# A second matmul front in split products: low parts by GpSimd, roots straight from PSUM

## The chip, the cores and the metric

The kernel runs on one core of one Trainium2 chip. The metric is the device time of one execution in microseconds. The kernel before was timed three times (2276.06, 2279.28 and 2283.34 us); the profile is of one more execution, which took 2286.72 us, of which the span of its instructions is 2284.9 us.

## The reference, cut to what matters

Two transformer layers run one after the other, all in fp32, on 256 tokens of width 1024. Each mixes the tokens and then sends them through an expert layer (PEER). The change is in the mixing part of the second layer, on 272 rows (16 meta rows are added):

```python
n = rmsnorm_2(h, norm_mix[l])
parts = jnp.split(n @ w_in[l], offsets, axis=-1)
c_q, c_kv, k_pe, gq, gk, gv, ga, gg, gate_a, gate_b = parts
y_a = mla_branch(c_q, c_kv, k_pe, ...)
y_b = gla_branch(gq, gk, gv, ga, gg, ...)
mix = jax.nn.sigmoid(gate_a) * (y_a @ w_o_mla[l]) + jax.nn.sigmoid(gate_b) * (y_b @ w_o_gla[l])
h = h + mix @ w_out[l]
...
# in mla_branch, for each of 8 heads
q_nope = rmsnorm_2(q[..., :MLA_NOPE], qn_nope)
q_pe = rope(rmsnorm_2(q[..., MLA_NOPE:], qn_pe), cos[:, None, :], sin[:, None, :])
k_nope = rmsnorm_2(kv[..., :MLA_NOPE], kn_nope)
...
# in gla_branch: log_a from ga, a causal scan with decay, then
return rmsnorm_2(o, g_norm).reshape(B, L, GLA_DV) * jax.nn.silu(gg)
```

## The kernel before, in words

**Weights.** All weights are cut into units of 128 x 1024 fp32 words (512 KB), one column block of a projection each, in the order of use. SyncE loads them into a ring of 4 slots; a slot is free for unit u + 4 when the last matmul of unit u is done. In the second layer's front the order is cq, ckv, kpe, gq, gk, ga, uq, ukv_k, ukv_v, gv (8 units), gg (8), gate_a (8), gate_b (8), wo_mla (8), wo_gla (8), w_out (8). Beside every third unit from gv on SyncE also writes one part of a zero fill to HBM.

**Two kinds of tile.** A tile is the product of one unit with 256 or 272 columns, 8 steps of 128 x 128, into one of 3 PSUM banks; a tile waits until the tile three before it has been taken out of its bank. A plain tile (`tile`, L930) multiplies fp32 words directly. A split tile (`split_tile`) uses a high part and a low part of weights and activations, and makes three passes for each step (L905 to L907: high by high, low by high, high by low). `split_weights` makes the parts: ScalarE casts the unit to a high part in one of three rotating buffers (L590; the cast waits for the last tile that used that buffer), and VectorE subtracts it from the unit, in place (L593). `split_at` hangs the cast and the subtraction of unit u on the tile of unit u - 2: `take_tiles` issues them just before it waits for that tile. In the kernel before, cq, ukv_v, gv, gg, gate_a and gate_b are plain; the other groups of this front are split.

**The order of the work.** Each engine has a queue written out by hand, in order, with semaphores between them. The stages of this front that the change touches:

1. Head norms of q (`norm_qn`, 8 groups, and `norm_qpe`, 4): per group TensorE sums squares (L1068, B_STAT banks in turn), VectorE scales and adds eps (L1080) and inverts (L1082), ScalarE takes the root (L1053), VectorE multiplies (L1099). VectorE inverts group g + 1 before it multiplies group g. The eight gv tiles lie between (`gv_fill`), each followed by three transposes (L970).
2. gg tiles 0 and 1, then the decay: four matmuls (L1821), `dve_gla_decay`, `act_gla_decay` (Exp L1858, Ln L1860).
3. Head norms of k (`norm_kn`, 8 groups), each with one tile beside it: gg 2 to 7 with Silu (L603), gate_a 0 and 1 with Tanh (L610). In group 0 VectorE also runs `dve_gla_sums` (L1837 to L1847), and ScalarE, after the tile of group 1, `act_gla_fades` (L1865 to L1868), which waits for those sums; in group 3 VectorE multiplies by the fades.
4. gate_a 2, two rope matmuls (L1566), gate_a 3, three more; then the first scores (L1642), which wait for the last rope step on VectorE.
5. Attention, 16 items. TensorE in item i: a decay level (L1955), one tile of gate_a 4 to 7 or gate_b (12 of the items have one), transposes of the probabilities (L1656), the scores of item i + 2, then the product with v (L1664), which waits for ScalarE's copy of the transposes. ScalarE in item i: the tile's casts, the tile's Tanh, the exponential of item i + 1 (L1725), that copy (L1742, L1745), and a decay exponential (L1944).
6. `gla_out`: wo_mla tiles beside the state products (L1979), the output products and the last norm.

GpSimd has little here: it zeroes some padding (L2727 to L2733). Its other work, the scatter of the expert gates, lies elsewhere.

Of the kernel before, what the change touches and what calls it, by code (L numbers as in the profile page):

```python
# [30 lines left out]
P = 128  # L31
# [232 lines left out]
def build(nc, stream, xc, metaT, vectors, common, consts1, consts2, keys1, keys2, w_a2, out):  # L264
# [142 lines left out]
    knope, knope_n = named("knope", HEADS, TM), named("knope_n", HEADS, TM)  # L407
    v2_flat = named("v2", 3 * D)
    v2 = v2_flat.rearrange("p (a d) -> p a d", a=3)
# [22 lines left out]
    kpe_pair = A2.take(2, TM)  # L432
# [5 lines left out]
    n2_hi, n2_lo = parted("n2_hi", "knope_n", KD, TM), parted("n2_lo", "v2", KD, TM)  # L438
# [4 lines left out]
    mixed2_hi, mixed2_lo = parted("mixed2_hi", "qnope", KD, T), parted("mixed2_lo", "v2", KD, T)  # L443
# [5 lines left out]
    whi_early, _ = place("whi_early", [P, WHI, UNIT], F32R, at=s_at)  # L449
    whi_a, _ = place("whi_a", [P, 1, UNIT], F32R, at=gbuf_at + whi_first)  # L450
# [22 lines left out]
    mixed2 = v2_flat[:, 0:KD * T].rearrange("p (k t) -> p k t", k=KD)  # L473
# [77 lines left out]
    def whi(j):  # L551

        if split_units[j] < units["wq1"][0]:
            return whi_front[:, j % WHI, :]
        if split_units[j] < units["wo_mla"][0]:
            return whi_early[:, j % WHI, :]
        m = (split_units[j] - units["wo_mla"][0]) % WHI
        return whi_a[:, 0, :] if m == 0 else whi_b[:, m - 1, :]

    def split_tile(group, unit, ready, hi, lo, cols, engine, take, k=KD, at=0, words=UNIT):  # L560

        if unit not in split_units:
# [6 lines left out]
            elif j < SPLIT_LEAD:  # L569
                split_at.setdefault(fill_at[FILL_SPLIT - SPLIT_LEAD + j], []).append(j)  # L570
            elif unit not in (units["ckv"][0], units["ckv"][1], units["wo_mla"][0], units["wo_mla"][1]):
# [9 lines left out]

    def split_weights(kind, eng, j):

        u, n = split_units[j], split_words[j]
        if kind == "act":
# [259 lines left out]
    for half, u in enumerate(units["ukv_v"]):  # L845
        for t, (a, n) in enumerate(KT2):
            pairs = [(ckvn[:, k, a:a + n], slot(u)[:, k * 512:(k + 1) * 512]) for k in range(2)]
            tile("ukv_v", u, None, pairs, n, 512, "act", v2_take(v2[0:n, t, half * 512:(half + 1) * 512], n))
# [9 lines left out]
    for i, u in enumerate(units["gv"]):  # L858
        tile("gv", u, None, std_pairs(u, n2), P, TM, "act", gv_take(i))
        gv_tile.append(len(tiles) - 1)  # L860
        gv_seq.append(taken["act"])
    group2("gg", silu_g, None, nT, T, make=lambda d: take_func(d, ACT.Silu))
    group2("gate_a", sgate_a, None, nT, T, make=take_gate)
    group2("gate_b", sgate_b, None, nT, T, make=take_gate)
    gates2_taken = taken["act"]

    def wo_mla_take(n):
        def f(kind, eng, src):
            if n == 0:
                eng.wait_ge(S("taken_act"), gates2_taken)  # L870
            return eng.scalar_tensor_tensor(mixed2[:, n, :], sgate_a[:, n, :], 1.0, src, ALU.add, ALU.mult)
# [2102 lines left out]
```

## Time and profile before

| | |
|---|---|
| three timed runs, median | 2279.28 us |
| the profiled execution, its own time | 2286.72 us |
| span of its instructions | 2284.9 us |
| TensorE busy | 2242.8 us, 98% |
| VectorE, ScalarE, GpSimd busy | 1694.2, 1298.4, 438.5 us |
| mean granted clock of TensorE | 0.996 of full speed |

The page of the profile gives the busy time of each engine, the span in 40 slices, and the chain of work that ended last, followed back from the last instruction. Matmuls are pipelined, so a busy TensorE isn't TensorE at its peak. Other views of the same trace are used too: the chain in order of time, the timeline of one engine, groups of instructions by line, and busy time by stretch. Times are microseconds from the start of the span.

### The profile page before, as it was taken

To read this page: it belongs to the slowest core of one execution; us is meant where nothing else is said; L and a number is where in the kernel's file an instruction comes from. 1 tells how busy PE (TensorE), PEld (TensorE's weight loads), DVE (VectorE), ACT (ScalarE), POOL (GpSimd) and SP (SyncE) were. 2 spreads that over 40 slices of the span, in tenths; PEclk is the share of its full clock that TensorE was granted. 3 is DMA by queue.
4 is the path that set the end of the run, shared out by engine and by line. 5 is a ranking of instruction groups with operands and counts; after the bars stand their busy time and mean duration, and the time that the engine had idled before them with its cause. 6 is when DMAs were issued, how large, how long until landed. Compare 5 with 4: busy or idle time off the path is not lost.

```text
span 2284.9 us, 47675 instructions
## 1 busy us (share of the span) xinstructions
PE 2242.8 (98%) x15260; PEld 2039.6 (89%) x15260; DVE 1694.2 (74%) x3690; ACT 1298.4 (57%) x2725; POOL 438.5 (19%) x269
## 2 busy tenths in 40 slices
PE   8999999999999999999999999999999999999999
PEld 2888899999999888888878789999999999888887
DVE  4787768888879777777658655768888788777776
ACT  3477455555577555555546334555555586555554
POOL 0000000767672000000000000001667681000000
PEclk9999999999999999999999999999999999999999
DMA  8767445777754666666455324555777755666665
GB/s 315 262 230 247 164 151 182 184 184 184 184 140 133 213 208 210 209 210 205 151 174 158 111 83 157 185 166 183 178 184 184 185 122 158 210 207 208 210 210 166
DMA packets 191117, 422.84 MB, mean 185 GB/s; under 512 B 54289, under 2 KB 88337, under 8 KB 190625
## 3 DMA queue, kind: packets, MB, share of 16 engines
q1 hardware_dynamic: 150112, 413.73, 54.8%
q0 software_dynamic: 36864, 0.15, 4.7%
q10 hardware_dynamic: 4032, 7.64, 0.9%
q8 instruction: 54, 0.88, 0.2%
q14 instruction: 55, 0.44, 0.1%
HBM read 403.48 MB, written 17.96 MB: 184 GB/s over the span
## 4 chain that ended last, share of the span: by engine, by line
PE 90%; DVE 4%; ACT 3%; DMA 2%; issue 1%; SPq 0%; POOL 0%; DVEq 0%; ACTq 0%; POOLq 0%
PE ps L2030 21%; PE ps L905 14%; PE ps L907 14%; PE ps L906 14%; PE ps L2031 10%; PE ps L930 10%; PE ps L2339 3%; DMA ring<-stream 2%; PE ps L1664 1%; PE ps L1642 1%; PE ps L2062 1%; PE ps L1955 1%; ACT arena L658 1%; DVE hl L2109 0%; PE ps L1068 0%
## 5 line engine op out<-in xcount | busy, mean ns | idle before, releaser
L2030 PE MATMUL ps<-csplit,hl 128*128 128x512 f32 x2048 | 725.4, 399 | 4.4 <-issue 3.5
L2263 POOL DMA_INDIRECT gates<-gbuf,picks_at x256 | 434.3, 1697 | 953.4 <-issue 520.0
L905 PE MATMUL ps<-hsplit,hl 128*128 128x256 f32 x2048 | 582.4, 284 | 0.0
L907 PE MATMUL ps<-hsplit,hl 128*128 128x256 f32 x2048 | 579.5, 283 | 0.0
L906 PE MATMUL ps<-hsplit,hl 128*128 128x256 f32 x2048 | 579.4, 283 | 0.0
L2031 PE MATMUL ps<-csplit,hl 128*128 128x256 f32 x2048 | 575.8, 281 | 0.0
L2106 ACT CAST hl<-ring 128x512 fp32r<-128x512 f32 x562 | 342.7, 619 | 298.9 <-PE ps L907 259.7
L2109 DVE TENSOR_TENSOR hl<-ring,hl 128x512 fp32r<-128x512 f32 x562 | 385.8, 693 | 125.2 <-ACT hl L2106 88.8
L2030 PEld LDWEIGHTS ps<-csplit,hl 128*128 128x128 f32 x2048 | 385.6, 188 | 101.4 <-issue 5.4
L2446 DVE TENSOR_TENSOR hl<-ring,hl 128x512 fp32r<-128x512 f32 x508 | 351.3, 692 | 74.8 <-ACT hl L2436 62.2
L906 PEld LDWEIGHTS ps<-hsplit,hl 128*128 128x128 f32 x2048 | 393.1, 192 | 0.0
L905 PEld LDWEIGHTS ps<-hsplit,hl 128*128 128x128 f32 x2048 | 393.0, 192 | 0.0
L907 PEld LDWEIGHTS ps<-hsplit,hl 128*128 128x128 f32 x2048 | 392.9, 192 | 0.0
L2031 PEld LDWEIGHTS ps<-csplit,hl 128*128 128x128 f32 x2048 | 387.6, 189 | 0.0
L2436 ACT CAST hl<-ring 128x512 fp32r<-128x512 f32 x508 | 314.1, 619 | 80.6 <-PE ps L2031 80.5
L2434 ACT CAST csplit<-arena 128x256 fp32r (+1 forms) x256 | 103.9, 407 | 243.2 <-DVE arena L2378 229.6
L2440 DVE TENSOR_TENSOR csplit<-arena,csplit 128x256 fp32r<-128x256 f32 x256 | 108.9, 426 | 131.3 <-ACT csplit L2434 131.3
L930 PE MATMUL ps<-arena,ring 128*128 128x256 f32 (+2 forms) x768 | 180.9, 390 | 4.0 <-DVE arena L758 2.4
L930 PEld LDWEIGHTS ps<-arena,ring 128*128 128x128 f32 x768 | 145.3, 191 | 30.4 <-issue 9.8
L2144 ACT ACTIVATE arena<-ps 128x256 f32<-128x256 f32 (+1 forms) x272 | 103.3, 380 | 18.6 <-PE ps L907 17.6
L2727 POOL MEMSET arena<- 128x544 f32 x1 | 0.6, 553 | 410.6 <-PE ps L907 410.6
L665 DVE TENSOR_REDUCE arena<-arena 128x128 f32<-128x1024 f32 x32 | 62.2, 1948 | 20.4 <-ACT arena L658 20.4
(379 smaller groups left out, 3162.2 us busy)
## 6 DMA issues: line engine op xcount, KB each, us to landing
ring<-stream SPq DMA_DIRECT2D x675, 512.0 KB
s_area<-stream SPq DMA_DIRECT2D x48, 512.0 KB, 4.9
gates<-zeros SPq DMA_DIRECT2D x32, 512.0 KB, 5.1
gring<-gates SPq DMA_DIRECT2D x256, 64.0 KB, 3.9
gates<-gbuf,picks_at POOLq DMA_INDIRECT x256
arena<-xc ACTq DMA_DIRECT2D x2, 1024.0 KB, 15.3
arena<-keys ACTq DMA_DIRECT2D x2, 1024.0 KB, 9.1
gbuf<-consts ACTq DMA_DIRECT2D x1, 1120.0 KB, 5.2
```

The lines of the kernel that those rows point to most:

```text
L905: pe.matmul(out_ap, w[0], m[0], start=start, stop=False)
L906: pe.matmul(out_ap, w[1], m[0], start=False, stop=False)
L907: return pe.matmul(out_ap, w[0], m[1], start=False, stop=stop)
L930: mm = pe.matmul(ps[0:t.rows, t.bank, 0:t.cols], lhs, rhs, start=(t.start and i == 0), stop=(t.stop and i == last))
L2030: pe.matmul(ps[:, bank, :], w_hi, m_both, start=start, stop=False)
L2031: return pe.matmul(ps[:, bank, 0:T], w_lo, m_both[:, 0, :], start=False, stop=stop)
L2106: eng.copy(hl[:, hslot, 0, :], raw).then_inc(S("split_hi"), 1)
L2109: eng.tensor_tensor(hl[:, hslot, 1, :], raw, hl[:, hslot, 0, :].bitcast(F32), ALU.subtract)\
L2263: pool.indirect_dma_start(out=cells, out_offset=bass.IndirectOffsetOnAxis(ap=picks_at[:, i, c:c + 1], axis=0), in_=gates[:, i, c:c + 1], i ...
L2436: eng.copy(hl[:, hslot, 0, :], slot(unit)[:, part]).then_inc(S("split_hi"), 1)
L2440: ins = eng.tensor_tensor(csplit[:, cslot, 1, :], acts[:, c], csplit[:, cslot, 0, :].bitcast(F32), ALU.subtract)
L2446: eng.tensor_tensor(hl[:, hslot, 1, :], slot(unit)[:, part], hl[:, hslot, 0, :].bitcast(F32), ALU.subtract).then_inc(S("split_lo"), 1)
```

## The change

All 32 units of gv, gg, gate_a and gate_b become split tiles. ScalarE still casts their high parts; their low parts are subtracted by GpSimd, which counts them on a semaphore of its own (`w_lo_pool`). (The change's title speaks of 35 units; cq's three stay plain in this diff.) To make room, v's values, a key buffer and the normalised keys move to other places. The head norms become a `HeadNorm`: ScalarE takes the root of the PSUM sum directly, with the scale and eps in the same instruction, VectorE inverts that, then multiplies; there is no longer an inversion ahead. The Silu of gg is left off until `act_gla_out`, one instruction over all eight tiles, and the Tanh of gate_a 0 to 3 until item 1 of the attention; those tiles are taken out by plain copies.

```diff
@@ buffers
+    whi_x, _ = place("whi_x", [P, UNIT], F32R, at=...)
+    whi_y, _ = place("whi_y", [P, UNIT], F32R, at=gbuf_at + G2.at)
+    whi_z, _ = place("whi_z", [P, UNIT], F32R, at=s_at + 3 * UNIT)
...
@@ whi(j)
+        if split_units[j] < units["gate_a"][0]:
+            return whi_early[:, j % WHI, :]
+        if split_units[j] < units["gate_b"][0]:
+            return (whi_x, whi_y, whi_z)[(split_units[j] - units["gate_a"][0]) % 3][:, :]
         if split_units[j] < units["wo_mla"][0]:
-            return whi_early[:, j % WHI, :]
+            return (whi_x, whi_y)[(split_units[j] - units["gate_a"][0]) % 2][:, :]
...
@@ split_weights
+    def low_by_pool(j):
+        return units["gv"][0] <= split_units[j] <= units["gate_b"][-1]
...
+        if kind == "dve" and low_by_pool(j):
+            return
...
-               .then_inc(S("w_lo"), 1)
+               .then_inc(S("w_lo_pool" if kind == "pool" else "w_lo"), 1)
...
@@ tiles
-        tile("gv", u, None, std_pairs(u, n2), P, TM, "act", gv_take(i))
+        split_tile("gv", u, None, *n2_parts, TM, "act", gv_take(i))
...
-    group2("gg", silu_g, None, nT, T, make=lambda d: take_func(d, ACT.Silu))
-    group2("gate_a", sgate_a, None, nT, T, make=take_gate)
-    group2("gate_b", sgate_b, None, nT, T, make=take_gate)
+    group3("gg", silu_g, None, n2T_parts, T)
+    gg_taken = taken["act"]
+    RAW_GATES = 4
...
+    def take_gate_a(dst):
+
+        made_gates.append(dst)
+        return take_copy(dst) if len(made_gates) <= RAW_GATES else take_gate(dst)
+    group3("gate_a", sgate_a, None, n2T_parts, T, make=take_gate_a)
+    group3("gate_b", sgate_b, None, n2T_parts, T, make=take_gate)
...
@@ HeadNorm, new, for norm_qn, norm_qpe and norm_kn
+        def act_roots(self, eng):
+            for g in range(len(self.groups)):
+                eng.wait_ge(S("norm_summed"), self.g0 + g + 1)
+                if g < 2:
+                    eng.wait_ge(S(self.before[g][0]), self.before[g][1])
+                else:
+                    eng.wait_ge(S(self.used), g - 1)
+                eng.activation(self.root[:, (self.g0 + g) % 2, 0:self.cols], ps[:, B_STAT[(self.g0 + g) % 2], 0:self.cols],
+                               ACT.Sqrt, scale=1.0 / self.width, bias=eps).then_inc(S("norm_rooted"), 1)
+                if self.fill:
+                    take_tiles("act", eng, self.fill[g])
+                if self.beside:
+                    self.beside("act", eng, g)
...
+        def pe(self, eng):
+            eng.wait_ge(S("norm_squared"), self.s0 + 1)
+            for g, group in enumerate(self.groups):
+                if g < 2:
+                    eng.wait_ge(S("norm_inverted"), self.g0 + g - 1)
+                else:
+                    eng.wait_ge(S("norm_rooted"), self.r0 + g - 1)
...
+        def dve(self, eng):
...
+            for g in range(len(self.groups)):
+                root = self.root[:, (self.g0 + g) % 2, 0:self.cols]
+                eng.wait_ge(S("norm_rooted"), self.r0 + g + 1)
+                eng.reciprocal(root, root).then_inc(S("norm_inverted"), 1)
+                if self.amid:
+                    self.amid(eng, g)
+                eng.wait_ge(S("norm_inverted"), self.g0 + g + 1)
+                for k in self.groups[g]:
+                    eng.scalar_tensor_tensor(self.dst(k), self.src[:, k, :], self.gain(k), root, ALU.mult, ALU.mult)\
+                       .then_inc(S(self.used if g < len(self.groups) - 1 else self.done), 1)
...
@@ act_att2_step and act_gla_out
+        if i == 1:
+            act.wait_ge(S("taken_act"), gg_taken + RAW_GATES)
+            raw = sgate_a[:, 0:RAW_GATES, :]
+            act.activation(raw, raw, ACT.Tanh, scale=0.5).then_inc(S("raw_gates_made"), 1)
...
     def act_gla_out(act):
+        act.wait_ge(S("taken_act"), gg_taken)
+        act.activation(silu_g, silu_g, ACT.Silu).then_inc(S("silu_made"), 1)
         act.wait_ge(S("gla_kept"), len(gla_steps))
         split_weights("act", act, first_out + 1)
...
@@ GpSimd's queue
-                    pool.wait_ge(S("tile_done"), group_of["ga"][-1] + 1)
-                    pool.memset(kpe_pair, 0.0)
                     pool.memset(pt2[:, :, 2 * P:], 0.0)
-                    pool.memset(v2[:, 2, :], 0.0).then_inc(S("pads_zeroed"), 1)
-                if b == 2:
+                    pool.wait_ge(S("tile_done"), group_of["ukv_k"][-1] + 1)
+                    pool.memset(v2_c, 0.0).then_inc(S("pads_zeroed"), 1)
+                    pool_split(pool, split_units.index(units["gv"][0]), split_units.index(units["gv"][-1]) + 1)
                     pool.wait_ge(S("qn_ready"), 1)
                     for t in range(NT):
                         ins = pool.memset(amat[t], 0.0)
                     ins.then_inc(S("amat_zeroed"), 1)
+                    last_of_pool = split_units.index(units["gate_b"][-1]) + 1
+                    first_gg = split_units.index(units["gg"][0])
+                    pool_split(pool, first_gg, first_gg + 2)
+                    pool.wait_ge(S("gv_kept"), 2)
+                    pool.memset(kpe_pair, 0.0).then_inc(S("pads_zeroed"), 1)
+                    pool_split(pool, first_gg + 2, last_of_pool)
```

The calls of `take_tiles` that the diff adds to VectorE's queue issue nothing, since every low part in those groups is GpSimd's.

## Rows read from the trace of the kernel before

**Rows 1.** The page: shares of the chain that ended last.

```profile
PE 90%; DVE 4%; ACT 3%; DMA 2%; issue 1%; SPq 0%; POOL 0%; DVEq 0%; ACTq 0%; POOLq 0%
```

**Rows 2.** By stretch: from:to, length, then busy us of each engine, PEclk the granted clock.

```profile
1228.00:1264.00 36.00, 35.47 (x163) 30.67 (x163) 31.88 (x49) 33.69 (x41) 0.00 (x0) 1.00 0.52 159
1264.00:1282.00 18.00, 15.10 (x67) 12.02 (x66) 12.12 (x35) 3.93 (x12) 0.00 (x0) 0.91 0.33 102
```

**Rows 3.** The chain in order of time, cq to gk: start us, us, what.

```profile
1101.61 10.36 PE ps L930 x48
...
1132.39 1.29 PE ps L1068 x6
1139.72 0.92 PE ps L1068 x4
```

**Rows 4.** The chain in order of time, gv to the first scores.

```profile
1191.44 3.67 PE ps L930 x16
...
1195.44 0.43 PE ps L1068 x2
...
1219.20 6.91 PE ps L930 x32
1226.11 2.04 PE ps L1821 x8
...
1244.52 0.72 PE ps L1068 x2
...
1269.94 2.59 issue
1272.54 3.50 PE ps L1642 x8
```

**Rows 5.** The chain in order of time: one attention item, and the start of wo_mla 1.

```profile
1276.04 3.47 PE ps L930 x16
1279.81 0.60 ACT gbuf L1725 x2
1280.87 0.94 PE ps L1664 x6
...
1282.70 3.47 PE ps L930 x16
...
1370.88 0.12 PE ps L905
```

**Rows 6.** Groups by line and shape, 1228 to 1264.

```profile
L1082 DVE RECIPROCAL gbuf<-gbuf 128x272 f32<-128x272 f32 x8 | 14.8, 1853 | 0.3
...
L1053 ACT ACT_TABLE_LOAD x8 | 10.3, 1283 | 0.1
...
L1099 DVE SCALAR_TENSOR_TENSOR arena<-arena,vec,gbuf 128x272 f32<-128x272 f32 x8 | 3.5, 439 | 2.5 <-ACT gbuf L1053 2.5
```

**Rows 7.** The timeline of ScalarE: start us, us, engine line op, [idle before, releaser].

```profile
1136.36 1.03 ACT L590 CAST whi_early<-ring 128x1024 fp32r<-128x1024 f32 x1
...
1222.97 2.01 ACT L1047 ACTIVATE arena<-arena 128x2176 f32<-128x2176 f32 x1
...
1232.47 1.11 ACT L1860 ACTIVATE gbuf<-gbuf 128x1088 f32<-128x1088 f32 x1
...
1241.77 1.06 ACT L1865 ACTIVATE arena<-gbuf 128x1024 f32<-128x1024 f32 x1
...
1367.97 2.00 ACT L590 CAST whi_b<-ring 128x1024 fp32r<-128x1024 f32 x2 [0.86 <-DVE arena L1930]
```

**Rows 8.** The timeline of VectorE: a low part, and the decay sums.

```profile
1131.37 1.23 DVE L593 TENSOR_TENSOR ring_lo<-ring,whi_early 128x1024 fp32r<-128x1024 f32 x1 [1.91 <-ACT whi_early L590]
...
1235.00 0.66 DVE L1837 TENSOR_SCALAR gbuf<-gbuf 128x1088 f32<-128x1088 f32 x1
...
1241.54 0.16 DVE L1847 COPY arena<-gbuf 128x4 f32<-128x4 f32 x1
```

**Rows 9.** The timeline of GpSimd.

```profile
1151.03 0.96 POOL L2729 MEMSET arena<- 128x1024 f32 x1
```

More of the change, by code:

```diff
@@ L570, in split_tile @@
                 split_at.setdefault(fill_at[FILL_SPLIT - SPLIT_LEAD + j], []).append(j)
+            elif unit in units["gv"][:SPLIT_LEAD]:
+                split_at.setdefault(group_of["ukv_v"][3 * units["gv"].index(unit)], []).append(j)
             elif unit not in (units["ckv"][0], units["ckv"][1], units["wo_mla"][0], units["wo_mla"][1]):
@@ L580, in split_tile, with low_count @@
         tiles[-1].split = j
+    def low_by_pool(j):
+        return units["gv"][0] <= split_units[j] <= units["gate_b"][-1]
+    def low_count(j):
+        return sum(low_by_pool(i) == low_by_pool(j) for i in range(j + 1))
     def split_weights(kind, eng, j):
         u, n = split_units[j], split_words[j]
+        if kind == "dve" and low_by_pool(j):
+            return
         if kind == "act":
@@ L1107, in dve, with __init__ @@
                     chain(ins, eng)
+    class HeadNorm(Norm):
+        def __init__(self, *args, used, before, **kw):
+            Norm.__init__(self, *args, **kw)
+            self.used, self.before = used, before
+        def act_roots(self, eng):
[18 more added lines that the diff above has]
+                    eng.wait_ge(S("norm_rooted"), self.r0 + g - 1)
+                for k in group:
+                    eng.matmul(ps[:, B_STAT[(self.g0 + g) % 2], 0:self.cols], self.lhs, self.squares[:, k, 0:self.cols],
+                               start=True, stop=True).then_inc(S("norm_summed"), 1)
+                if self.fill:
+                    pe_tiles(eng, self.fill[g])
+                if self.beside:
+                    self.beside("pe", eng, g)
+        def dve(self, eng):
+            for r in self.ready:
+                wait(eng, *r)
+            for g in range(len(self.groups)):
[8 more added lines that the diff above has]
+                       .then_inc(S(self.used if g < len(self.groups) - 1 else self.done), 1)
@@ L1478, in fades_in_kn @@
             act_gla_fades(eng)
-    norm_kn = Norm(knope, sq2, HEADS, TM, flat_groups(HEADS), ones, P, rs2, [("taken_act", uk_taken), ("norm_summed", 19)],
-                   lambda k: v_("kn_nope"), dst=lambda k: knope_n[:, k, :], done="kn_ready", fill=pieces([group_of["gg"][2:], group_of["gate_a"][:2]], HEADS),
+    norm_kn = HeadNorm(knope, sq2, HEADS, TM, flat_groups(HEADS), ones, P, rs2, [("taken_act", uk_taken), ("norm_summed", 19)],
+                   lambda k: v_("kn_nope"), dst=lambda k: knope[:, k, :], done="kn_ready", used="kn_scaled", before=[("qpe_scaled", 3), ("qpe_ready", 1)], fill=kn_fill,
                    beside=fades_in_kn, amid=decay_in_kn)
@@ L2715, in _, with pool_split @@
             sp.wait_ge(S("out_stored"), 48)
+        def pool_split(pool, first, end):
+            for j in range(first, end):
+                split_weights("pool", pool, j)
         @block.gpsimd
```

56 lines of the change are left out of this document (37 added, 19 removed).

## The prediction

> **What bounds the kernel now.** I read the page first: 90% of the chain that ended last is TensorE [rows 1]. The split into stretches says where that holds: in the k norms (1228 to 1264) TensorE is busy 35.47 of 36 us, but ScalarE 33.69 and VectorE 31.88 too, so three engines are nearly full at once; from 1264 to 1282 TensorE is busy 15.10 of 18 at a mean clock of 0.91 [rows 2]. The chain in order of time then shows what a tile costs and which waits stand between tiles [rows 3 to 5]: through the q norms nothing but TensorE; one wait for VectorE near 1244.52; 2.59 us of idleness before the first scores, which wait for the last rope step; and in each attention item a stretch in which ScalarE carries the chain. So the ceiling of this change is TensorE's own saving, and the question is how much of it the other queues give back.
>
> **Step 1, the matmuls.** Two split tiles of 272 columns (gk) fill 1133.68 to 1139.72, 3.02 each. Between 1111.97 (1101.61 + 10.36) and 1132.39 lie three more of them (ckv, kpe) and four of 256 (gq): (20.42 - 9.06) / 4 = 2.84 each [rows 3]. A plain tile takes 3.67 at 272 columns and 3.45 at 256 (6.91 for two) [rows 4]. The ceiling is 8 x 0.65 + 24 x 0.61 = 19.8 us, 0.9%.
>
> **Step 2, the parts.** 32 casts of 1.03 us on ScalarE [rows 7], 32 subtractions on GpSimd. No row shows a GpSimd instruction that reads. Below, it can't be shorter than the one pass that writes 1024 words, 0.96 us [rows 9]; above I take three such passes (two operands and the result), 2.9. I take two passes, 1.9: VectorE's own subtraction, 1.23 [rows 8], is the nearest row and above the lower end, and 1.9 lies between it and the upper one. The Trainium skill (GPSIMD Engine Reference, Performance versus the Vector engine) gives about 2.6 cycles a word for a two-input operation at 1.2 GHz, an estimate of 2.2 us here; the sum would be 0.3 us longer by it. TensorE takes 2.84 us or more for a unit, so GpSimd isn't the bound in steady state at any value up to 2.9; it costs only where a cast comes late.
>
> **Step 3, the q norms.** From the last ukv_v tile on, TensorE has 8 tiles, 8 x 0.33 of transposes (1195.11 to 1195.44) and 12 sums of 0.43 [rows 4]. Casts for gv are issued two tiles ahead and their buffers are free, ScalarE has time (two casts, two takes and three roots, some 4 us in each 8), and VectorE's group (1.85 + 0.44 at the most [rows 6]; three of them 6.9 in TensorE's 2 x 3.35 + 3 x 0.43 = 8.0) keeps up. The full 8 x 0.65 = **-5.2** is kept. Cover: if VectorE is slowed by more than 0.35 us a group, it becomes the bound.
>
> **Step 4, the k norms.** Here HeadNorm's order matters. Before, TensorE's third sum waits for VectorE's inversion of group 0, and VectorE does groups 0 and 1 before the decay sums, whatever ScalarE is at. Now the third sum waits for ScalarE's root of group 0, and in ScalarE's queue that root stands behind the decay's Exp and Ln; the cast of gg 4 stands behind the root. I lay the queues out from the end of the last transpose (1219.20 before), t = 0:
> - gg 0 and 1 end at 5.7, the logits at 7.7 (2.04 [rows 4]). VectorE has |a| ready 1.85 later, 9.55. ScalarE: Exp 10.7, table 12.0, Ln 13.1, table 14.4, root 14.85 (1.11 each [rows 7], 1.28 a table [rows 6]).
> - TensorE has done sum, gg 2, sum, gg 3 at 14.3. It waits 0.55 for the root; then gg 4 waits for its cast (15.8) and subtraction (17.7): 2.4 us idle.
> - VectorE inverts group 0 (16.7), runs the decay sums (6.7 from 1235.00 to 1241.70 [rows 8]) to 23.4. ScalarE's fades take 1.8 (1.06 for the first 1024 words of some 1600 [rows 7]), a table 1.28, so the root of group 2 comes at 26.95. TensorE, at 23.85 with gg 5, waits 3.1 for it, sums, then waits 2.4 more for gg 6 (cast 27.9, subtraction 29.8).
> - After that nothing is late: five tiles and three sums, 15.6, end gate_a 2 at 45.4. Before, that was at 44.5: 1244.52, four sums and five tiles of 3.45 [rows 4].
>
> So -0.61 x 9 of tiles turned into **+0.9**: about 8.5 us of new idleness. The 16 table loads that the raw copies take away (some 20 us of ScalarE) buy nothing here, as TensorE didn't wait for them. From gate_a 2 to the scores one tile is shorter: **-0.6**. Such waits also cost clock: after 2.59 us of idleness the first score matmuls took 3.50 us [rows 4], and the granted clock of that stretch, 0.91 over 18 us, is 1.6 us short of full [rows 2], as if it had stood at 1.2 GHz in place of 2.4 for 3.3 us. I charge 1.7 us once: the first drop is swallowed by the wait for the root of group 2, the second isn't: **+1.7**.
>
> **Step 5, attention.** An item with a tile takes 6.66 us (1276.04 to 1282.70): 3.47 of tile, then 1.36 until the product with v starts (take, exponential 0.60, copies), then 0.94 and 0.89 [rows 5]. gate_b has two cast buffers, x and y, and its casts are issued two tiles ahead: the cast for unit u + 2 waits for the tile u, the very tile whose end starts the 1.36 us, and stands before its take in ScalarE's queue. It pushes exponential and copies back by 0.97 (two in a row take 2.00, one 1.03 [rows 7]). That holds in 8 of the 12 items (gate_a 6 and 7, gate_b 0 to 5): 2.84 + 1.36 + 0.97 + 0.94 + 0.89 = 7.00, +0.34 each; the other four save 0.63. Together **+0.2** where the tiles alone would give -7.6. The Tanh of 128 x 1024 in item 1 lies in ScalarE's idle time.
>
> **Step 6, the Silu.** One instruction of 128 x 2048, 1.9 to 2.0 us by the square of 128 x 2176 [rows 7], with a table load of 1.28, stands before the cast of wo_mla 1, which began at 1367.97 [rows 7]; ScalarE was idle for 0.86 before it. The cast moves to 1370.4 (1367.1 + 3.3), its subtraction ends 1.03 + 1.23 later, at 1372.7 at the latest, and TensorE began that tile at 1370.88 [rows 5]: **+1.7**.
>
> **Without a cost:** the moved pads (0.5 to 1 us of GpSimd, asked for long after), the moved arrays, SyncE (slots come free earlier; about 131 GB/s of weights is wanted in the q norms at one unit in 4.0 us).
>
> **The sum:** -5.2 + 0.9 - 0.6 + 1.7 + 0.2 + 1.7 = -1.3 us. The profiled execution, 2286.72 with a span of 2284.9, would come to 2285.4; it stands 7.4 above the median of the timed runs, 2279.28, from which I forecast **2278 us**. With GpSimd at 0.96 it is 1 us less, at 2.9 one more.
>
> **The rivals.**
> - *GpSimd and VectorE hinder each other* (slower). The trace has no GpSimd read beside VectorE, so the price lies between nothing and the whole of each subtraction. If a VectorE instruction with two SBUF operands must wait until a running subtraction ends, then in the q norms the multiply of L1099 waits on some eight of them, each up to 1.9 less what the inversion covers: laid out in the same way, the last transpose comes 4.1 us later than in step 3. In the k norms the decay sums are such instructions back to back: GpSimd and VectorE hold each other up, and the scores come 1.6 later still. The four items without a tile follow upon a late exponential, some 0.6 each, and one more clock drop 1.7: +9.8 in all, 2287. With a subtraction of 2.3 the same layout gives +16, 2293, and at 2.9 GpSimd and VectorE together become the bound, over 2300 (the range stops short of it). It decides from about 0.35 us a group on. For it: VectorE is 31.88 of 36 busy in the k norms [rows 2]. Against it: nothing in the trace. The Trainium skill (SBUF — State Buffer, Who interferes with whom) says just this: a VectorE instruction with two SBUF inputs contends with a GpSimd instruction that reads SBUF, and the later one blocks fully. No run here shows it yet; by that rule this rival is what happens.
> - *The stalls of step 4 don't arise and the casts of step 5 are hidden* (faster): only the Silu stands against 19.8, so -18, 2261; with one of the two, about 2269. For it: all 19.8 us are on the chain now. Against it: the queue orders are in the code, and the same laying out of the queues for the kernel before puts the fifth k sum and the scores within 1 us of where the trace has them (1244.52, 1272.54).
> - *Something late in the ring*: casts wait for weights, as both zero fills and units share the queue; each late unit in the k norms costs its lateness, some 3 to 10 us in all, 2280 to 2287.
>
> **Chances.** Forecast 0.44; hindrance 0.36; faster rival 0.12; late weights 0.08. About 0.3% (6.8 us) is what a measurement can tell from no change, so faster is below 2272.4, slower above 2286.1. The forecast lies within (0.38; 0.04 faster, 0.02 slower), hindrance is mostly slower (0.30, 0.06 within), late weights split evenly. Faster 0.16, same 0.48, slower 0.36. The range goes from 2269 (one of the two stalls absent) to 2294 (hindrance at 2.3 us); the forecast's own is 2274 to 2283.
>
> **What would show it.** GpSimd's subtractions: 32 rows, 1 to 2.9 us apart at their closest. In the q norms a gv tile every 4.0 us on average. In the k norms TensorE idle before gg 4, before the fifth sum and before gg 6, 2.4 to 3.1 us each, and granted clock below 1 there. In attention, items of 7.0 us with a cast right after a tile's end and of 6.0 without. A Silu at the head of `act_gla_out` and wo_mla 1 late by 1.7. Hindrance would show as multiplies of L1099's successor that start late or take over 1 us while GpSimd runs. The prediction is wrong if the last transpose comes less than 4 or more than 6.5 us earlier, or if the items' length doesn't split in two as said.

## The result and the profile after

The changed kernel takes 2301.74 us (median of 4 runs, 2298.05 to 2308.18), the kernel before beside it 2280.47 (4 runs, 2276.06 to 2283.34): a ratio of 1.0101, with a 95% interval of 1.0074 to 1.0128. It is about 1% slower. I had forecast 2278 and a range up to 2294. The profiled execution has a span of 2306.4 us.

The page, its shares of the chain that ended last; beside [rows 1] VectorE has grown:

```profile
PE 88%; DVE 6%; ACT 3%; issue 2%; DMA 1%; POOL 0%; DVEq 0%; ACTq 0%; POOLq 0%
```

Busy time by stretch, in the columns of [rows 2] (TensorE, its weight loads, VectorE, ScalarE, GpSimd, clock):

```profile
1171.00:1228.00 57.00, 48.07 (x287) 38.51 (x286) 43.69 (x32) 27.75 (x46) 26.15 (x14) 0.94 0.43 138
1228.00:1264.00 36.00, 26.23 (x160) 23.60 (x160) 25.46 (x32) 21.88 (x30) 16.04 (x7) 0.81 0.35 117
1264.00:1282.00 18.00, 13.65 (x108) 13.03 (x107) 17.86 (x11) 7.72 (x13) 10.52 (x5) 1.00 0.66 204
```

The stretches are the same times, not the same work: from 1264 to 1282 the changed kernel is still in its k norms. Where [rows 2] had TensorE at 35.47 of 36 us it now has 26.23, and from 1264 to 1282 VectorE is busy 17.86 of 18 with 11 instructions. Four of these are inversions, five are multiplies and two apply the fades; at the durations that they had before (1.85 and 0.44 [rows 6], 1.2 and at most 0.8) they would need about 12 us. The timeline of VectorE in the q norms (start us, us, engine line op) shows what fills it:

```profile
1191.93 1.75 DVE L1186 RECIPROCAL gbuf<-gbuf 128x256 f32<-128x256 f32 x1
1193.71 0.48 DVE L1191 SCALAR_TENSOR_TENSOR arena<-arena,vec,gbuf 128x256 f32<-128x256 f32 x1
1194.11 1.75 DVE L1186 RECIPROCAL gbuf<-gbuf 128x256 f32<-128x256 f32 x1
1195.89 2.52 DVE L1191 SCALAR_TENSOR_TENSOR arena<-arena,vec,gbuf 128x256 f32<-128x256 f32 x1
1198.34 1.74 DVE L1186 RECIPROCAL gbuf<-gbuf 128x256 f32<-128x256 f32 x1
1200.12 2.56 DVE L1191 SCALAR_TENSOR_TENSOR arena<-arena,vec,gbuf 128x256 f32<-128x256 f32 x1
```

And GpSimd's, same stretch:

```profile
1195.78 2.36 POOL L618 TENSOR_TENSOR ring_lo<-ring,whi_early 128x1024 fp32r<-128x1024 f32 x1 [6.35 <-ACT whi_early L615]
1200.00 2.40 POOL L618 TENSOR_TENSOR ring_lo<-ring,whi_early 128x1024 fp32r<-128x1024 f32 x1 [1.86 <-ACT whi_early L615]
```

The same multiply takes 0.48 us when GpSimd is idle and 2.52 when it starts 0.11 us behind a subtraction of 2.36: it ends 0.27 after the subtraction. Six of the twelve multiplies of the q norms are held like that, four of them for the whole 2.5 us. Lay the two timelines side by side: a held instruction shows as a long one, not as a wait. The reciprocals don't change. By kind, in the stretch of the q norms and the decay sums (busy us, mean ns of one):

```profile
L1186 DVE RECIPROCAL gbuf<-gbuf 128x256 f32<-128x256 f32 x12 | 20.9, 1746 | 1.6 <-ACT gbuf L1158 1.4
L1191 DVE SCALAR_TENSOR_TENSOR arena<-arena,vec,gbuf 128x256 f32<-128x256 f32 x12 | 15.9, 1328 | 0.4
L1505 DVE SCALAR_TENSOR_TENSOR resid<-resid,vec,arena 128x256 f32<-128x256 f32 x8 | 7.5, 1013 | 14.7 <-ACT arena L1499 14.7
...
L1930 DVE TENSOR_SCALAR gbuf<-gbuf 128x1088 f32<-128x1088 f32 x1 | 2.0, 2043 | 0.0
L1921 DVE TENSOR_SCALAR gbuf<-ps,vec 128x272 f32<-128x272 f32 x4 | 1.8, 498 | 4.0 <-PE ps L1914 4.0
```

This reaches TensorE, whose sums wait for the inversions and the roots behind the held multiplies. Its waits in the q norms (engine, line, what it waited for: us in total, times, longest), of which the kernel before has none:

```profile
PE ps L1173 <- DVE gbuf L1186: 5.6, 2, 3.4
PE ps L1173 <- ACT gbuf L1158: 2.1, 2, 1.9
```

To place the loss I use four marks, counted from the start of the first ukv_v tile, since that start itself moves by up to 11 us between executions: the start of the last transpose of the q norms, of the first scores, of the last product with v, and of the first sum of the GLA norm. Times are ratios to the kernel before on the same chip, with their 95% intervals.

| kernel | last transpose | scores | last product | norm | time |
|---|---|---|---|---|---|
| before | 47.9 | 101.5 | 195.0 | 224.9 | 1 |
| changed | 54.8 | 122.2 | 217.1 | 249.0 | 1.0101 (1.0074 to 1.0128) |
| e1 low parts by VectorE | 45.3 | 105.1 | 200.7 | 232.6 | 1.0022 (1.0004 to 1.0040) |
| e2 GpSimd only writes | 42.8 | 100.9 | 195.8 | 227.7 | 1.0015 (1.0000 to 1.0030) |
| e3 old norms | 48.6 | 112.7 | 208.7 | 240.6 | 1.0062 (1.0038 to 1.0086) |
| e4 before + HeadNorm | 47.9 | 106.4 | 198.4 | 228.3 | 1.0008 (0.9984 to 1.0032) |
| e5 four pieces | 43.6 | 104.5 | 198.7 | 230.6 | 1.0012 (0.9990 to 1.0034) |
| e6 old norms, GpSimd in k norms alone | 51.6 | 115.2 | 209.7 | 243.1 | 1.0059 (1.0035 to 1.0084) |
| e7 e1 + late casts | 46.7 | 108.7 | 201.0 | 232.9 | 1.0028 (1.0007 to 1.0050) |
| e8 e7 + old norms | 51.6 | 117.0 | 210.2 | 242.1 | 1.0066 (1.0043 to 1.0089) |
| e9 e5 + late casts | 43.5 | 105.4 | 193.0 | 224.9 | 0.9995 (0.9976 to 1.0013) |
| e10 e9 + old norms | 48.1 | 111.1 | 197.3 | 229.2 | 1.0015 (0.9995 to 1.0034) |
| e11 e10 + Silu moved | 48.1 | 111.1 | 197.4 | 227.3 | 1.0011 (0.9993 to 1.0029) |
| e12 e9 + Silu moved + root first | 43.5 | 99.2 | 186.7 | 216.6 | **0.9951** (0.9933 to 0.9968) |
| e13 e12, GpSimd only writes | 42.8 | 89.9 | 174.5 | 204.5 | 0.9902 (0.9880 to 0.9925) |
| e14 before + HeadNorm + root first | 47.9 | 102.4 | 196.1 | 226.0 | 1.0001 (0.9988 to 1.0014) |

The changed kernel loses 6.9 us in the q norms, 13.8 from there to the scores (67.4 against 53.6), 1.4 in attention and 2.0 behind it: 24.1 at the norm, 23 us by the ratio. Kernels that are alike up to a mark agree there within 1 us, except e1 and e7 (1.4 and 3.6 apart), so a single difference below 4 us before the scores says little.

### The profile page after: what moved, and what is told of

It reads as the page before. It is cut to its first block, busy times and chain, and to the rows that moved or that the text cites. A ratio compares the mean times of both kernels' runs of the same rounds, so it can differ in the third digit from the quotient of the medians.

```text
span 2306.4 us, 48254 instructions
## 1 busy us (share of the span) xinstructions
PE 2231.0 (97%) x15516; PEld 2040.8 (88%) x15516; DVE 1729.4 (75%) x3670; ACT 1314.4 (57%) x2746; POOL 515.5 (22%) x301
## 4 chain that ended last, share of the span: by engine, by line
PE 88%; DVE 6%; ACT 3%; issue 2%; DMA 1%; POOL 0%; DVEq 0%; ACTq 0%; POOLq 0%
PE ps L2125 21%; PE ps L939 15%; PE ps L941 15%; PE ps L940 15%; PE ps L2126 10%; PE ps L964 5%; PE ps L2434 2%; PE ps L1753 1%; DVE gbuf L1186 1%; DVE arena L1191 1%; DMA ring<-stream 1%; PE ps L2157 1%; PE ps L1731 1%; PE ps L2048 1%; ACT arena L683 1%
## 5 line engine op out<-in xcount | busy, mean ns | idle before, releaser
L940 PE MATMUL ps<-n_hi,ring_lo 128*128 128x256 f32 (+1 forms) x352 | 102.7, 292 | 0.0
L2473 DVE TENSOR_TENSOR arena<-arena,gring 128x128 f32 (+1 forms) x256 | 72.8, 285 | 2.9 <-DMA gring<-gates 2.9
```

Source lines behind the costliest of these rows:

```text
L940: pe.matmul(out_ap, w[1], m[0], start=False, stop=False)
```

## The experiments

### Is it GpSimd's reading? (e1 to e4)

e1: VectorE subtracts all 32 low parts, GpSimd none.

```diff
 def low_by_pool(j):
-    return units["gv"][0] <= split_units[j] <= units["gate_b"][-1]
+    return False
```

> The changed kernel with one difference: all 32 low parts of gv, gg, gate_a and gate_b are subtracted by VectorE (1.23 us each), GpSimd does none. Theory HOLD (a GpSimd subtraction and a VectorE instruction with SBUF inputs shut each other out; this costs nearly all of the +21 us): the multiplies of the q norms are back at 0.48 us, the last transpose of the q norms ends about 1213.5 in place of 1225.3; the k norms are set by VectorE (1.84 + 0.48 + 1.23 = 3.55 a group against 3.27 of TensorE), scores near 1275, in all 2275 to 2287 us. Theory QUEUES (the loss is HeadNorm's missing inversion ahead and casts that come late, whichever engine subtracts): the gaps in TensorE stay, scores at 1288 or later, in all 2293 to 2305 us.

e2: GpSimd is kept as long but only writes.

```diff
+    elif kind == "pool":
+        eng.wait_ge(S("w_hi"), j + 1)
+        low = low_of(u).bitcast(F32)
+        for again in range(2):
+            eng.memset(low[:, 0:n], 1e-4).then_inc(S("pool_again"), 1)
+            eng.wait_ge(S("pool_again"), 2 * (low_count(j) - 1) + again + 1)
+        eng.memset(low[:, 0:448], 1e-4).then_inc(S("w_lo_pool"), 1)
```

> The changed kernel with GpSimd's 32 subtractions replaced by three memsets each over the same words (1024, 1024 and 448 words), which keep GpSimd about as long (2.35 us) but read nothing. The low parts of gv, gg, gate_a and gate_b are therefore a constant, so the output isn't the reference's. All waits stay. Theory HOLD with its cause in GpSimd's reads: VectorE's multiplies take 0.48 us beside GpSimd, the last transpose of the q norms ends at 1213.5 to 1214.5, the scores near 1273, in all 2277 to 2282 us. Theory QUEUES (a low part that comes 2.35 us after its cast, and HeadNorm's order, make the loss): no change, 2298 to 2306 us. If GpSimd's writes alone hold VectorE too, 2298 to 2306 us as well, but with multiplies of 1 to 2.5 us.

e3 and e4 take HeadNorm out of the changed kernel, and put it alone into the kernel before.

```diff
-    norm_qn = HeadNorm(..., used="qn_scaled", before=[...])
+    norm_qn = Norm(...)        # e3: so for qpe and kn too; e4 is the reverse on the kernel before
```

> The changed kernel with the head norms of the kernel before (VectorE scales and adds eps, inverts one group ahead, ScalarE takes the root, VectorE multiplies) in place of HeadNorm; the 32 split units with their low parts by GpSimd stay. Theory HOLD: VectorE has one more instruction a group (0.3 to 0.4 us) but its multiply is held as before, so the time stays within 6 us of the changed kernel, 2296 to 2308 us, and multiplies still take about 2.5 us. Theory QUEUES: the inversion one group ahead takes the roots out of the way, TensorE's gaps in the k norms go, 2280 to 2290 us.

> The kernel before with HeadNorm alone: all of gv, gg, gate_a and gate_b stay plain, GpSimd subtracts nothing, Silu and Tanh stay where they were. Theory HOLD: TensorE stays the bound in the q norms; in the k norms the roots wait behind the decay's Exp and Ln as I laid out, a few us at most: within -1 and +6 us of the kernel before, 2279 to 2286 us. Theory QUEUES: HeadNorm makes a good part of the +21 us by itself, 2288 us or more.

e2 settles the cause. The groups of VectorE and GpSimd in the q norms of e2:

```profile
L1193 DVE RECIPROCAL gbuf<-gbuf 128x256 f32<-128x256 f32 x12 | 21.0, 1749 | 3.8 <-ACT gbuf L1165 3.8
L1198 DVE SCALAR_TENSOR_TENSOR arena<-arena,vec,gbuf 128x256 f32<-128x256 f32 x12 | 5.8, 485 | 0.4
L1512 DVE SCALAR_TENSOR_TENSOR resid<-resid,vec,arena 128x256 f32<-128x256 f32 x8 | 3.3, 481 | 14.7 <-ACT arena L1506 14.7
...
L620 POOL MEMSET ring_lo<- 128x1024 f32 x25 | 23.8, 953 | 25.5 <-ACT whi_early L615 24.8
L622 POOL MEMSET ring_lo<- 128x448 f32 x12 | 5.7, 472 | 0.7
```

GpSimd is as long at work (2.4 us a unit), the semaphore waits are as they were, and the multiply is back at 485 ns from 1328. TensorE's waits in the q norms fall from 7.7 us to 0.5:

```profile
PE ps L1180 <- ACT gbuf L1165: 0.5, 1, 0.5
```

The norm mark comes 21.3 us earlier and the time falls from 1.0101 to 1.0015, so some 20 of the 23 us are GpSimd's reads beside VectorE. Writing alone doesn't hold the multiplies. It isn't without effect, though: beside the MEMSETs a TENSOR_SCALAR of the decay sums took 1.53 us (0.73 in the kernel before), and a pair of MEMSETs 2.4 to 2.5 us in place of 1.96. VectorE and GpSimd in e2:

```profile
1232.07 0.66 DVE L1937 TENSOR_SCALAR gbuf<-gbuf 128x1088 f32<-128x1088 f32 x1
1234.09 1.53 DVE L1939 TENSOR_SCALAR gbuf<-gbuf 128x1088 f32<-128x1088 f32 x1
1231.16 2.46 POOL L620 MEMSET ring_lo<- 128x1024 f32 x2 [6.47 <-ACT whi_early L615]
1234.09 2.42 POOL L620 MEMSET ring_lo<- 128x1024 f32 x2
```

That is 0.8 us once, against 20 for the reads. e1 agrees from the other side: 1.0022, though VectorE carries 32 subtractions more, so the time is not in who has the work but in the two reading at once. (Its last transpose came at 45.3, not near 43.)

e3 lies between what the two theories said: 2295.75 us, by the ratios 9 us less than the changed kernel, where HOLD allowed 6 and QUEUES asked for 12 or more. Its multiplies in the q norms took 866 ns on the mean, against 1328 in the changed kernel: four of twelve are held, 1.6 to 2.1 us long, where the changed kernel has six, four of them of 2.5 us. e4 came out as HOLD had it, 1.0008; most of its 4.9 us before the scores is the root that stands behind Exp and Ln (TensorE waits 3.7 us for it, and e14 below, which moves that root, gives back 4.0).

### How long does the hold last, and what else is on the path? (e5 to e8)

e5: the same subtraction in four instructions.

```diff
-            eng.tensor_tensor(low_of(u)[:, 0:n], slot(u)[:, 0:n], whi(j)[:, 0:n].bitcast(F32), ALU.subtract)\
+            step = n // 4 if kind == "pool" else n
+            for a in range(0, n - step, step):
+                c = slice(a, a + step)
+                eng.tensor_tensor(low_of(u)[:, c], slot(u)[:, c], whi(j)[:, c].bitcast(F32), ALU.subtract)
+            c = slice(n - step, n)
+            eng.tensor_tensor(low_of(u)[:, c], slot(u)[:, c], whi(j)[:, c].bitcast(F32), ALU.subtract)\
                .then_inc(S("w_lo_pool" if kind == "pool" else "w_lo"), 1)
```

> The changed kernel with each of GpSimd's 32 subtractions cut into four instructions of 256 words; words, order and waits are otherwise the same, and the result too. All marks here and below count from the start of ukv_v: 47.9 (last transpose of the q norms), 101.5 (first scores), 195.0 (last product with v), 224.9 (last norm) in the kernel before, 54.8, 122.2, 217.1, 249.0 in the changed one. Theory HOLD-TO-THE-END (a VectorE instruction with SBUF inputs waits for the end of the GpSimd instruction that runs, not of all its work): a multiply waits for one piece of about 0.6 us at most, marks 43 to 46 and 103 to 110, 2282 to 2292 us. Theory SHARE (VectorE and GpSimd share the way to SBUF, and the amount of words counts): no change, marks near 55 and 122, 2298 to 2306 us; if each piece costs a start of its own, later.

VectorE's timeline in e5:

```profile
1197.11 0.57 DVE L1196 SCALAR_TENSOR_TENSOR arena<-arena,vec,gbuf 128x256 f32<-128x256 f32 x1
1197.60 1.74 DVE L1191 RECIPROCAL gbuf<-gbuf 128x256 f32<-128x256 f32 x1
1199.38 0.89 DVE L1196 SCALAR_TENSOR_TENSOR arena<-arena,vec,gbuf 128x256 f32<-128x256 f32 x1
```

And GpSimd's:

```profile
1195.09 2.30 POOL L621 TENSOR_TENSOR ring_lo<-ring,whi_early 128x256 fp32r<-128x256 f32 x3
1197.36 0.91 POOL L623 TENSOR_TENSOR ring_lo<-ring,whi_early 128x256 fp32r<-128x256 f32 x1
1199.26 2.31 POOL L621 TENSOR_TENSOR ring_lo<-ring,whi_early 128x256 fp32r<-128x256 f32 x3 [0.99 <-ACT whi_early L615]
```

GpSimd moves the same words and takes longer for them (2.8 us a unit where nothing disturbs it, 3.0 to 3.6 in the q norms and up to 4.3 in the k norms, against 2.35 to 2.6), yet the multiply falls to 0.48 to 0.93 us and the time to 1.0012, 20 us less than the changed kernel. The hold lasts to the end of one GpSimd instruction, so four short ones let VectorE in between. SHARE, which asked for no change, falls. The multiply at 1197.11 began inside one piece and ended 0.3 us behind the start of the next, and that next piece took 0.91 us in place of 0.72, what a piece takes alone: the two engines take turns.

e6 and e8 tried where and with which norms the subtractions cost; e7 tried step 5's cast.

```diff
 def low_by_pool(j):                                  # e6, with the old norms
+    return units["gg"][0] <= split_units[j] <= units["gate_a"][3]
@@ Attention.act                                     # e7, e8; low parts by VectorE as in e1
-    take_tiles("act", eng, self.fill[i])
+    take_tiles("act", eng, self.fill[i], "takes" if self.parts else None)
     ... exponential of item i + 1, copies of item i
+    if self.parts:
+        take_tiles("act", eng, self.fill[i], "casts")
```

> The changed kernel with the old norms, and with GpSimd's subtractions only in the stage where VectorE is full: gg 0 to 7 and gate_a 0 to 3. The low parts of gv, gate_a 4 to 7 and gate_b are subtracted by VectorE. Theory HOLD: no held multiply in the q norms, mark of the last transpose 43 to 45.5 (48.6 with GpSimd); from there to the scores still 62 to 65 as in the run with old norms and GpSimd throughout (64.1), so scores at 105 to 110; in all 2284 to 2292 us. If gv's 8 subtractions by VectorE (1.2 us each) cost as much as GpSimd's, the mark stays at 48.

> The changed kernel with all low parts by VectorE, as before in e1, and with ScalarE's casts in attention placed behind the exponential and the copies of the same item in place of ahead of the tile's take. Step 5 said that a cast that waits for the very tile pushes the product with v back by 0.97 in 8 of 12 items. If so: items of 7.0 us become 6.0 to 6.1, the stretch from the first scores to the last product with v falls from 95.6 to 87 or 88 us, in all 6 to 8 us less than with the casts ahead (2285.7), 2278 to 2280 us. Rival: VectorE's subtraction, now later by 1.4 us, holds up the mask of the next item; then 93 us or more and no gain.

> As the run with late casts, all low parts by VectorE, and the old norms in place of HeadNorm. Beside GpSimd's subtractions the old norms were 9.5 us faster up to the scores (112.7 against 122.2), in the kernel before HeadNorm alone costs 4.9 us up to the scores (106.4 against 101.5). Theory HEADNORM COSTS BY ITSELF (its root stands behind the decay's Exp and Ln): scores at 99 to 102, in all 2273 to 2277 us. Rival, VECTORE FULL: the old norms give VectorE 0.4 us more in each of 20 groups, and with the subtractions it is the bound in the k norms (0.4 + 1.85 + 0.4 + 1.2 = 3.9 a group against TensorE's 3.3): scores at 105 to 110, 2280 us or more.

e6 missed: the last transpose came at 51.6, not 43 to 45.5. With the old norms (2.6 us a group) and 1.16 for a gv subtraction VectorE's instructions stand nearly without a gap through the q norms (one of 0.43 us), and it is the bound. So VectorE full, not the hold, makes that mark, and e6 says little of the hold. e8 has the same 51.6 with nothing subtracted by GpSimd, and the rival VECTORE FULL holds there. e7 gave what step 5 said of ScalarE and no time: the items fell from 7.05 to 6.05 us, but the four-item rhythm kept one of 4.74 us in place of 2.91, where VectorE sat in front of a late subtraction with the next item's work behind it. The rival named that.

### With GpSimd in pieces (e9 to e11)

e9 joins e5's pieces with e7's late casts; e10 adds the old norms; e11 moves the Silu:

```diff
 def act_gla_out(act):
-    act.activation(silu_g, silu_g, ACT.Silu).then_inc(S("silu_made"), 1)
     act.wait_ge(S("gla_kept"), len(gla_steps))
     ...
     take_tiles("act", act, group_of["wo_mla"][1:4])
+    act.activation(silu_g, silu_g, ACT.Silu).then_inc(S("silu_made"), 1)
```

> The changed kernel with GpSimd's subtractions in four pieces, and with ScalarE's casts in attention behind the exponential and the copies of the same item. In the run with late casts and VectorE's subtractions TensorE's wait for ScalarE's copy fell from 10.7 us (10 times) to 2.8 (4), but VectorE sat 1 to 3 us in front of each subtraction with the next item's scaling and mask behind it, so only 3 us came out. GpSimd has nothing else to do. If step 5's cast is the cost and nothing else: the stretch from the first scores to the last product with v falls from 94.2 to 87 or 88 us, marks 43.6, 104.5, 192, 224, in all 6 us under four pieces alone (1.0012), 0.9975 to 0.9995 of the kernel before. Rival: a low part that comes 2.35 to 3 us after a late cast is too late for the tile of the next item: 93 us or more, no gain.

> The same with the old norms in place of HeadNorm. Theory HEADNORM'S ORDER (its third sum waits for a root that stands behind the decay's Exp and Ln; 5 us by itself in the kernel before, where VectorE had no subtractions): the stretch from the last transpose to the first scores falls from 60.9 us to 54 to 56, mark of the scores 97 to 100, in all 0.995 to 0.998. Rival, VECTORE FULL (old norms with VectorE's subtractions gave 117 against 108.7 for HeadNorm): VectorE has 0.42 + 1.85 + 0.6 = 2.9 us a group here against TensorE's 3.3, so it should not be; if held multiplies of 0.9 are the rule it is, and the scores come at 104 or later.

> The same again with the one Silu of gg moved behind the takes of wo_mla 1 to 3 in ScalarE's queue, where ScalarE sat idle for 5.25 us in the changed kernel. Step 6 said that the Silu pushes wo_mla 1 back by 1.7; from the last product with v to the last norm the changed kernel takes 31.9 us, the kernel before 29.9. Expected: 29.9 to 30.2, in all 1 to 2 us less than the run without this move. Rival: Silu and its table load now hold up the copies of the state products; then no gain.

TensorE's waits in attention, in the changed kernel (engine, line, what it waited for: us in total, times, longest):

```profile
PE ps L1753 <- ACT gbuf L1834: 11.9, 13, 1.1
PE ps L1731 <- issue: 2.6, 1, 2.6
```

and in e9:

```profile
PE ps L1762 <- ACT gbuf L1843: 1.7, 2, 1.1
```

e9 met its sizes: from the scores to the last product 87.6 us against 94.2, 6.6 less, where 6 to 7 was said. The items are 6.05 us. Its time, 0.9995, sits at the upper edge of what I expected. e11 gave back 1.9 us at the norm (197.4 to 227.3 is 29.9, as before); 1.0011 against 1.0015 is too little to see in the times. e10 refuted me: the old norms are worse with split weights, 48.1 and 111.1. ScalarE's timeline at the start of the q norms of e10 shows why:

```profile
1181.25 0.41 ACT L1508 ACTIVATE arena<-arena 128x256 f32<-128x256 f32 x1
1187.23 0.42 ACT L1098 ACTIVATE gbuf<-gbuf 128x256 f32<-128x256 f32 x1 [5.57 <-DVE gbuf L1127]
1187.56 1.03 ACT L615 CAST whi_early<-ring 128x1024 fp32r<-128x1024 f32 x1
```

The first root waits 5.57 us for VectorE's inversion, and the cast of gv 2 stands behind it. In e9 the root waits for TensorE's sum and not for VectorE, and it came at 1179.26, 11.7 us behind the start of ukv_v against 17.3. HeadNorm's worth here is that it takes VectorE out of ScalarE's way.

### Order in the k norms (e12 to e14)

In e9 ScalarE's timeline in the k norms reads:

```profile
1227.72 0.50 ACT L1167 ACTIVATE gbuf<-ps,small 128x272 f32<-128x272 f32 x1
...
1229.45 1.28 ACT L1969 ACT_TABLE_LOAD   x1
1238.39 1.06 ACT L1969 ACTIVATE arena<-gbuf 128x1024 f32<-128x1024 f32 x1 [7.66 <-DVE arena L1951]
...
1240.23 1.28 ACT L1167 ACT_TABLE_LOAD   x1
1241.52 0.49 ACT L1167 ACTIVATE gbuf<-ps,small 128x272 f32<-128x272 f32 x1
1241.91 1.03 ACT L615 CAST whi_early<-ring 128x1024 fp32r<-128x1024 f32 x1
```

The fades wait 7.66 us for VectorE's sums, and the root of group 2 and the cast of gg 6 stand behind them. e12 changes that order:

```diff
+    norm_kn.act_root(act, 0)               # ahead of Exp and Ln
     act_gla_decay(act)
+    take_tiles("act", act, kn_fill[0])
@@ take_tiles, after the take of a tile
+    for j in cast_after.get(n, ()) if kind == "act" else ():   # gg 4 to gate_a 3: unit u + 3
+        split_weights(kind, eng, j)
@@ ScalarE
-    if kind == "act" and g == 1:           # act_gla_fades
+    if kind == "act" and g == 2:
@@ VectorE: dve_gla_sums behind the multiply of group 0, not ahead of it
```

> The changed kernel with four pieces and late casts (0.9995; marks 43.5, 105.4, 193.0, 224.9), the Silu moved behind the takes, and another order in the k norms alone: ScalarE takes the first root before the decay's Exp and Ln (it sat idle there for 2.5 us), casts gg 4 to gate_a 3 right behind the take of the tile three before, and runs the fades one group later; VectorE scales group 0 before the decay sums. In the run with late casts TensorE waited 8 to 9 us for gg 6, whose cast stood behind the root of group 2, which stood behind the fades and the sums. Laid out from that trace's rows: sums start at 1224.8 in place of 1228.5, the last multiply of the k norms comes at 1256 in place of 1262, set by VectorE (2.65 a group, 9.7 of sums, 3.3 of fades). Theory ORDER: from the last transpose to the scores 55 to 57 in place of 61.9, marks 99 and 217 to 219, 0.995 to 0.998 in all. Rival, VECTORE FULL from end to end: order gains nothing beyond 1 us, 0.998 to 1.000.

> The same, but GpSimd's 32 subtractions replaced by three memsets each, as in the earlier run that only writes; the low parts are a constant, so the output isn't the reference's. It shows what GpSimd's reads still cost once they are cut up and the order is mended. If VectorE sets the end of the k norms in the run above, sums (6.7 for 9.7) and multiplies (0.48 for 0.8) give back 4 to 6 us up to the scores: mark 94 to 96, 0.992 to 0.996. If what is left are ScalarE's and TensorE's own waits, less than 2 us.

> The kernel before (all 32 units plain, nothing on GpSimd, Silu and Tanh where they were) with HeadNorm and the same order of root, sums and fades in the k norms. HeadNorm alone gave 106.4 up to the scores and 58.5 from the last transpose to them, against 101.5 and 53.6 for the old norms. If the 4.9 us were the root behind Exp and Ln: 53 to 54.5, time as before (0.998 to 1.000). If the gain of the reordered split kernel is one of order alone, this kernel shows it as well: below 53, 0.996 or less.

e12 is faster than both kernels: 0.9951, 2270.69 us against 2281.53 beside it. Scores at 99.2 as laid out, 216.6 at the norm. TensorE's waits up to the scores, in e9:

```profile
PE ps L944 <- issue: 7.9, 2, 4.6
PE ps L1182 <- ACT gbuf L1167: 1.7, 2, 0.8
PE ps L1182 <- DVE gbuf L1195: 0.5, 1, 0.5
```

and in e12:

```profile
PE ps L1192 <- ACT gbuf L1181: 4.8, 1, 4.8
PE ps L947 <- issue: 1.3, 1, 1.3
PE ps L1674 <- DVE arena L1210: 0.9, 1, 0.9
```

With two of 0.5 and 0.3 us more in e12, these waits come to 10.1 us and 7.8, only 2.3 less, while the scores come 6.2 us earlier. The rest is the clock: from the last transpose to the scores TensorE runs the same matmuls, busy 49.0 us in e9 at a granted clock of 0.88 and 45.2 in e12 at 0.96. So more than half of what the order buys is that TensorE, with one wait of over 3 us in place of two, is slowed less afterwards.

e14 (1.0001) says that the order alone gives the plain kernel nothing; the gain needs the split tiles too. e13 shows what the reads still cost in pieces: 9.3 us up to the scores, where I expected 4 to 6, and 0.9902, at a granted clock of 1.00 up to the scores. The scans of the decay sums show it, 696 ns for one of 128 words in e12 against 403 in e13:

```profile
L1956 DVE TENSOR_TENSOR_SCAN gbuf<-onesbuf,gbuf 128x128 f32<-128x128 f32 x8 | 5.3, 696 | 0.0
```

(e12), and e13:

```profile
L1958 DVE TENSOR_TENSOR_SCAN gbuf<-onesbuf,gbuf 128x128 f32<-128x128 f32 x8 | 2.9, 403 | 0.0
```

With no reads on GpSimd the norm mark is 20.4 us ahead of the kernel before: a gain of the size of step 1's ceiling, 19.8, can get through the other queues once nothing is read beside VectorE.

## Why the prediction was wrong, step by step

- **The failing step is the overlap in step 3: that GpSimd's subtractions run beside VectorE at no cost, in the q norms and after them.** Step 3 said that VectorE keeps up, added "if VectorE is slowed by more than 0.35 us a group, it becomes the bound", and the sum has no term for it. In the runs held multiplies take 2.5 us in place of 0.48, and the reads cost 20 of the 23 us (changed against e2). The mechanism stood in the first rival, so the choice between it and the forecast was wrong too: against it I set only that the trace held no such pair, which is no evidence, and gave it 0.36. The Trainium skill (SBUF — State Buffer, Who interferes with whom) says that a VectorE instruction with two SBUF inputs contends with a GpSimd instruction that reads SBUF, and that the later one is blocked until the other is done; the changed trace agrees (2.52 beside 2.36). The rival was also mis-sized: +9.8 at 1.9 us and +16 at 2.3 (which make 2288 and 2294, not 2287 and 2293), while the reads cost 20 us at 2.35 to 2.6. In the layout I let only the q norms' multiplies and the sums wait; in the trace multiplies of the k norms (1.42 us on the mean of eight), the scaling by `once` (7.5 us in place of 3.3) and the rope steps wait too.
- **Step 1** held: 5.1 us over 8 gv tiles in e2 are 0.64 a tile, 0.65 forecast.
- **Step 2**: a subtraction took 2.35 to 2.6 us, one 2.9 (I took 1.9, bounds 0.96 and 2.9; the row of [rows 8] for VectorE is not a near row for GpSimd). The estimate from the 2.6 cycles a word of the Trainium skill (GPSIMD Engine Reference, Performance versus the Vector engine) was 2.2, nearer. By itself the difference costs little, as e2 has the same length.
- **Step 3** as it stood: -5.2 forecast; e2, without the reads, has -5.1. With them +6.9, outside the 4 to 6.5 earlier that I had named as the bound of being right.
- **Step 4**: the three idle spans are there in e2 (3.3 and 2.8 us ahead of gg 4 and gg 6, 1.1 for the root of group 2), with 0.5 for the root of group 0: 7.7 us, where 8.5 was laid out. Still e2 has +4.5 where +0.9, -0.6 and +1.7 make +2.0. Right in mechanism, 2.5 short, and the term is the clock: e2's granted clock from 1228 to 1264 is 0.86, 5.0 us short of full, and I charged 1.7 (in the changed kernel it is 0.81, 6.8 us). The closing line of the step counts 9 tiles; up to gate_a 2 there are 11, and the layout above it has them all, so +0.9 stands. With the reads it is +13.8.
- **Step 5** held in kind: eight items of 7.03 to 7.06 us (7.00 forecast), the others with a tile 6.05 to 6.33. But an item behind one without a tile had been 6.56, not 6.66, and three of those without a tile went from 2.91 to some 3.46, as the first rival had it (3.04 in e2, so most of that is the reads). +1.4 in place of +0.2; late casts (e9) take the whole of it away.
- **Step 6**: +1.7 forecast, +2.0 measured in the changed kernel and gone with the move in e11.

The forecast's own sum, -1.3, is what e2 tests: its marks say +2.8 and its ratio 1.0015. Without the reads the sum was 4.1 us short, nearly all of it in step 4's clock and step 5; with them another 20 are missing, and those are the one term that stood at nothing.

Of the other rivals, the faster one did not come: the stalls of step 4 and the long items of step 5 are both there. Late weights did not come either: from 1165 to 1400 the profile puts no wait of TensorE, ScalarE or GpSimd in the changed kernel down to a load.

Open: why the multiply's hold costs the old norms less (e3) isn't tested apart from their other order; and how far smaller pieces than 256 words would go wasn't tried.

## What to carry to other kernels

Before work that reads SBUF goes to GpSimd, list the VectorE instructions beside it of the forms that were held here (two tensors from SBUF, or a TENSOR_SCALAR from SBUF to SBUF), and charge each one that starts during a GpSimd instruction the rest of that instruction; a trace that holds no such pair is silence, not evidence. If the work must go there, cut it into short instructions (four of 256 words gave back 20 us here). Then look at what stands behind each wait in ScalarE's in-order queue: e12's last 4.4 parts in 1000 (the Silu's move is at most 1 of them) came from putting a root and the casts ahead of a wait for VectorE, and more than half of the gain up to the scores is TensorE's clock (busy 49.0 us in e9, 45.2 in e12).

## What the runs showed of the hardware

- A VectorE instruction with two tensors from SBUF that starts behind a GpSimd subtraction is held to the end of it: 2.52 us for a multiply of 0.48 beside a subtraction of 2.36. A TENSOR_SCALAR with one tensor from SBUF and its result there was held too, 2.04 us in place of 0.66 [rows 8]. The same form reading PSUM (498 ns) and RECIPROCAL (1746 ns) are untouched.
- The hold goes both ways: in pieces, one of GpSimd's took 0.91 us beside a multiply, 0.72 alone (e5).
- GpSimd's MEMSET of 128x1024 words (0.97 us) holds neither the multiply (485 ns) nor RECIPROCAL (1749 ns), but a TENSOR_SCALAR of 128x1088 from SBUF to SBUF took 1.53 us beside one, 0.73 in the kernel before, and two MEMSETs took 2.46 us around another such TENSOR_SCALAR, 1.96 alone (e2).
- GpSimd's subtraction of 128x1024 words takes 2.35 to 2.6 us, twice VectorE's 1.23 [rows 8]; in four pieces 2.8 undisturbed and up to 4.3 beside VectorE.
- In the same stage of the same matmuls TensorE was busy 45.2 us at a granted clock of 0.96 and 49.0 at 0.88 (e12, e9).
